# Hybrid decoder step on one core: attention outputs turned by transposes after a GpSimd add, in place of fp32 products with [I;I]

## The chip, the core and the metric

The kernel runs on one core of a Trainium2 chip. The metric is the device time of one launch in microseconds. The engines of the core are TensorE (PE; its weight loads are listed as PEld), VectorE (DVE), ScalarE (ACT), GpSimd (POOL) and SyncE (SP), each with its own queue of instructions; they wait for each other by semaphores.

## What is computed

One decoder layer over a prompt of 2048 positions and over 8 sequences of 8 new positions with a paged cache of 8192. The change touches the attention of the prompt alone: 8 heads of 64, causal, with a forget-gate term in the logits.

```python
def _attend_block(q, k, v, qc, kc, q_pos, k_pos):
    s = jnp.einsum('bqhd,bkhd->bhqk', q, k).astype(jnp.float32) * ATTN_SCALE
    s = s + jnp.swapaxes(qc, 1, 2)[..., :, None] - jnp.swapaxes(kc, 1, 2)[..., None, :]
    causal = (q_pos[:, None] >= k_pos[None, :])[None, None]
    s = jnp.where(causal, s, NEG_INF)
    p = jax.nn.softmax(s, axis=-1)
    return jnp.einsum('bhqk,bkhd->bqhd', p.astype(v.dtype), v)

# _layer
p = x @ w_in                      # q, k, v, forget gates, pooling channels
att = _forget_attention(...)      # 128 queries at a time
mix = concat(att, pool) @ w_out
x1 = layer_norm(ALPHA * x + mix)
x2 = layer_norm(ALPHA * x1 + conv_ffn(x1))
```

## The kernel before, in words

Stages run one after the other with a barrier of all engines between them: projection (A), gates and pooling (B), prompt attention (C), mixing and first norm (Dp), the feed-forward network with the decoding attention beside it (F, N), and the sampled rows (S). The change is in `stage_attention` (C).

It works on 32 groups (`groups`): a head `h` and a block `g` of 512 queries, four tiles of 128. Even heads take g = 0, 1, 2, 3, odd heads 3, 2, 1, 0, so that the lengths repeat every eight groups. A group has 4, 8, 12 or 16 turns, one for each tile of 128 keys (`turns`, `steps`, 320 in all). Orders are fixed by hand in each engine's block; two turns make a `pair`.

- TensorE: `logits` writes the products q.k of a coming group into PSUM (`ps_s`, lines 880 to 884); `transposes` turns tiles of the exponentials (`row`) so that keys lie on partitions (`ps_t`, line 896); `times_v` multiplies by the values into `ps_o` (lines 908 and 910), once with the rounded weights `p_hi` and once with the rest `p_lo`; `turn_back(n)` brings the group's output into rows of queries.
- VectorE: `copy_logits` (line 949) scales, copies and takes the least value; `rest` (line 961) forms `p_lo`; `normalise` (lines 968 to 978) multiplies the turned output by the reciprocal sum into `att`.
- ScalarE: `exp` (line 1005), `high` (line 1013, rounds to `p_hi`), and `o_out` (line 1019), the copy of `ps_o` to SBUF.
- GpSimd has nothing to do in this stage.

`v` holds, for each key, the 64 values of a head as a rounded part and a rest side by side, 128 columns. `ps_o` therefore has the rounded values' output on partitions 0 to 63 and the rest's on 64 to 127; their sum is the output. Before, `o_out` copies all 128 partitions to `oT` (in the persistent tile `raw0`, seen as `X_raw` in the profile), and `turn_back` multiplies each 128x128 block of `oT` by `both`, two 64x64 identities on top of each other: this fp32 product adds the halves and turns them at once, into 64 columns per tile of queries.

At the border between groups n and n+1, ScalarE waits in `o_out(n)` for the last `times_v` of n and copies; behind it stand exponentials and roundings of the coming turns. TensorE goes on with two turns of transposes and with logits, waits for the copy at the first `times_v` of n+1 (`o_copied`), does two turns of `times_v`, and then `turn_back(n)` (`nat_at`). VectorE's `normalise(n)` waits for it (`nat_done`). The buffers of `ps_t` are four and are used in turn (`t_free`).

## Time and profile before

| | us |
|---|---|
| median of 3 runs | 3110.25 (3105.86 to 3114.26) |
| span of the profiled execution | 3104.8 |
| TensorE busy | 2980.9 (96%) |
| VectorE busy | 2011.5 (65%) |
| ScalarE busy | 1554.0 (50%) |
| GpSimd busy | 810.0 (26%) |

The profile is of one execution; for it only the span is given, from its first to its last recorded instruction, and no time around it. Busy times are sums over the engine's instructions. Matmuls overlap in the records, since they are pipelined: a matmul lasts longer there than the distance to the next one. An idle time in square brackets behind a row is what the engine waited just before it, with the operation that ended the wait. The granted clock is a share of TensorE's full clock (1.0 is 2.4 GHz, 0.5 is 1.2 GHz), averaged over a stretch. The prompt attention spans about 481 to 966 us.

### The profile page before, as it was taken

Reading aid. Unit: us, or ns where it says so; the run is one execution under the profiler, and the core shown is the slowest. Engines: PE = TensorE matmul, PEld = TensorE weight load, DVE = VectorE, ACT = ScalarE, POOL = GpSimd, SP = SyncE. Lnnn points to the kernel's source line nnn. Section 1 sums busy time; section 2 is a strip of 40 time slices with the busy share of each in tenths; the row PEclk is TensorE's granted clock in tenths of the full one; section 3 lists DMA queues with packets and bytes.
Section 4 is the critical chain, followed back from the end, with each engine's and each line's share of the span. In section 5 each row is a group of like instructions: output and inputs, shape, how many; then the busy total and the mean of one; then the engine's idle time right before and its main releaser. Section 6 shows DMA issues by size and latency. Waiting matters only on the chain. (4 is left out here: it accounts for less than half of the span.)

```text
span 3104.8 us, 57063 instructions
## 1 busy us (share of the span) xinstructions
PE 2980.9 (96%) x19424; PEld 2376.2 (77%) x19424; DVE 2011.5 (65%) x4185; ACT 1554.0 (50%) x3113; POOL 810.0 (26%) x1437
## 2 busy tenths in 40 slices
PE   8999978999999997999999999999999999999988
PEld 8999966777777886777777777777777777777762
DVE  5433336787886655866678666678666678666445
ACT  3111115776775113466445666446676446766424
POOL 1101110000000103434444334454343454442300
PEclk9999988999999998999999999999999999999999
DMA  5444455322303356757877677787677887775868
GB/s 205 134 127 122 127 133 152 81 55 67 86 21 112 122 166 219 253 197 247 289 270 262 235 247 246 268 298 269 222 245 230 284 299 240 249 240 177 301 249 323
DMA packets 270120, 626.51 MB, mean 202 GB/s; under 512 B 52279, under 2 KB 116695, under 8 KB 261855
## 3 DMA queue, kind: packets, MB, share of 16 engines
q1 hardware_dynamic: 169271, 305.32, 30.9%
q0 software_dynamic: 93760, 296.83, 28.2%
q10 hardware_dynamic: 6800, 20.71, 2.1%
q8 instruction: 156, 2.56, 0.3%
q14 instruction: 133, 1.09, 0.1%
HBM read 555.52 MB, written 67.33 MB: 201 GB/s over the span
## 5 line engine op out<-in xcount | busy, mean ns | idle before, releaser
L1568 PE MATMUL F_ps_u<-X_x_hi,F_w_hi 128*128 128x512 f32 x1408 | 577.4, 410 | 10.9 <-DVE F_w_lo L1827 10.9
L1569 PE MATMUL F_ps_u<-X_x_lo,F_w_hi 128*128 128x512 f32 x1408 | 560.0, 398 | 0.0
L1570 PE MATMUL F_ps_u<-X_x_hi,F_w_lo 128*128 128x512 f32 x1408 | 559.8, 398 | 0.0
L1827 DVE TENSOR_TENSOR F_w_lo<-X_raw,F_w_hi 128x512 fp32r<-128x512 f32 x352 | 239.2, 681 | 269.9 <-ACT F_w_hi L1727 268.2
L2056 POOL DMA_DIRECT2D N_dec<-cache_k x512 | 278.1, 543 | 312.5 <-issue 192.9
L2096 POOL DMA_DIRECT2D N_dec<-cache_v x512 | 281.9, 551 | 285.0 <-issue 163.7
L1568 PEld LDWEIGHTS F_ps_u<-X_x_hi,F_w_hi 128*128 128x128 f32 x1408 | 266.7, 189 | 103.5 <-issue 34.9
L1727 ACT CAST F_w_hi<-X_raw 128x512 fp32r<-128x512 f32 x352 | 214.3, 609 | 256.0 <-PE F_ps_y L1570 230.8
L1884 DVE STREAM_TRANSPOSE N_dec<-N_dec 128x1024 f32<-128x1024 f32 x256 | 303.6, 1222 | 19.2 <-DMA N_dec<-cache_k 18.8
L1570 PEld LDWEIGHTS F_ps_u<-X_x_hi,F_w_lo 128*128 128x128 f32 x1408 | 266.3, 189 | 64.5
L1569 PEld LDWEIGHTS F_ps_u<-X_x_lo,F_w_hi 128*128 128x128 f32 x1408 | 267.3, 190 | 56.7
L1752 ACT ACTIVATE F_h<-F_ps_u,F_coef 128x512 f32<-128x512 f32 x176 | 121.3, 689 | 344.6 <-PE F_ps_u L1570 344.5
L949 DVE TENSOR_SCALAR_CACHE_REDUCE C_row<-C_ps_s 128x512 f32<-128x512 f32 (+2 forms) x320 | 185.7, 609 | 81.6 <-PE C_ps_s L881 62.8
L252 PE MATMUL A_ps_p<-A_w_hi,A_x_hi 128*128 128x412 f32 (+1 forms) x640 | 226.0, 353 | 0.0
L2066 POOL DMA_DIRECT2D F_forget<-sc_wT x256 | 137.4, 542 | 332.1 <-DVE F_tops L1918 329.9
L254 PE MATMUL A_ps_p<-A_w_hi,A_x_lo 128*128 128x412 f32 (+1 forms) x640 | 223.7, 349 | 0.0
L253 PE MATMUL A_ps_p<-A_w_lo,A_x_hi 128*128 128x412 f32 (+1 forms) x640 | 223.5, 349 | 0.0
L1827 DVE TENSOR_TENSOR F_w_lo<-F_raw,F_w_hi 128x512 fp32r<-128x512 f32 x176 | 119.3, 678 | 126.6 <-ACT F_w_hi L1727 126.0
L1294 POOL TENSOR_TENSOR H_qs<-Dp_pin,H_qs 128x512 fp32r<-128x512 f32 x16 | 23.2, 1449 | 681.5 <-ACT H_qs L1216 681.5
L1013 ACT CAST C_p_hi<-C_ps_t 128x512 fp32r<-128x512 f32 (+1 forms) x320 | 151.7, 527 | 93.0 <-PE C_ps_t L896 92.9
L1568 PE MATMUL F_ps_y<-F_w_hi,F_g_hi 128*128 128x512 f32 x480 | 197.6, 412 | 0.0
L1570 PE MATMUL F_ps_y<-F_w_hi,F_g_lo 128*128 128x512 f32 x480 | 190.1, 396 | 0.0
(345 smaller groups left out, 6388.3 us busy)
## 6 DMA issues: line engine op xcount, KB each, us to landing
N_dec<-cache_k POOLq DMA_DIRECT2D x512, 256.0 KB, 3.6
N_dec<-cache_v POOLq DMA_DIRECT2D x512, 256.0 KB, 4.7
X_raw<-w_up_t SPq DMA_DIRECT2D x120, 512.0 KB, 5.2
F_raw<-w_up_t SPq DMA_DIRECT2D x56, 512.0 KB, 5.0
X_raw<-w_down SPq DMA_DIRECT2D x56, 512.0 KB, 5.4
sc_qk<-A_early SPq DMA_DIRECT2D x16, 1024.0 KB, 5.1
F_forget<-sc_wT POOLq DMA_DIRECT2D x256, 64.0 KB, 3.0
F_raw<-w_down SPq DMA_DIRECT2D x32, 512.0 KB, 4.3
```

The costliest lines, as they stand in the source:

```text
L252: nc.tensor.matmul(out, x_hi[:, t % 2, c, :], w_hi[:, c, cols], start=c == 0, stop=False)
L253: nc.tensor.matmul(out, x_hi[:, t % 2, c, :], w_lo[:, c, cols], start=False, stop=False)
L254: last = nc.tensor.matmul(out, x_lo[:, t % 2, c, :], w_hi[:, c, cols], start=False, stop=c == DC - 1)
L949: nc.vector.tensor_scalar(row[:, n % 2, r, o:o + w], ps_s[:, p % SBANKS, 0:w], -SCALE, None, ALU.mult, ALU.min, accum_out=least[:, n % 4, ...
L1568: nc.tensor.matmul(out, a_hi, b_hi, start=first, stop=False)
L1569: nc.tensor.matmul(out, a_hi, b_lo, start=False, stop=False)
L1570: return nc.tensor.matmul(out, a_lo, b_hi, start=False, stop=last)
L1727: nc.scalar.copy(w_hi[:, q % 4, :], raw[unit % RAW][:, q % 2 * 512:(q % 2 + 1) * 512]).then_inc(hi_done, 1)
L1827: nc.vector.tensor_tensor(w_lo[:, q % 4, :], raw[q // 2 % RAW][:, q % 2 * 512:(q % 2 + 1) * 512], w_hi[:, q % 4, :].bitcast(F32), ALU.subt ...
L1884: nc.vector.transpose(kt[:, :, half % 2 * 64:(half % 2 + 1) * 64].rearrange("p f (j t) -> p j f t", j=2), kin[:, half % KR, :, :].rearrang ...
L2056: pool.dma_start(kin[:, half % KR, j, :], io["cache_k"][ds(pages[j], 1), :, :].rearrange("a t c -> (a t) c"))\
L2096: pool.dma_start(vin[j:P:4, n % 2, :, :], io["cache_v"][ds(pages[j], 1), :, :].rearrange("a (b t) c -> (a t) b c", b=4))\
```

## The change

`o_out` copies the two halves of `ps_o` apart, both to partitions 0 to 63: the first to `oT`, which now has 64 partitions, the second to the new tile `oT_low`. A GpSimd block, new in this stage, adds `oT_low` into `oT` for each group and signals `o_summed`. `turn_back` waits for that sum and turns it by four transposes with the 64x64 corner of the identity, which write the same 64 columns per tile as before. Between its two copies ScalarE waits until the sum of the group before is done, since `oT_low` has a single buffer. The tile `both`, its two loads and their semaphore go.

```diff
@@ stage_attention
-        oT = persist["raw"][0][:, :].rearrange("p (a d) -> p a d", a=2)
-        both = m.sb("both", [P, HD])
+        oT = persist["raw"][0][0:HD, :].rearrange("p (a d) -> p a d", a=2)
+        oT_low = m.sb("oT_low", [HD, 512])
...
         @block.sync
         def _(sp):
-            sp.dma_start(both[0:HD, :], io["c_ident"][0:HD, 0:HD]).then_inc(c_in, 16)
-            sp.dma_start(both[HD:P, :], io["c_ident"][0:HD, 0:HD]).then_inc(c_in, 16)
...
             def turn_back(n):
                 tk = nat_tick[n]
-                if n == 0:
-                    pe.wait_ge(c_in, 32)
-                pe.wait_ge(o_copied, n + 1)
+                pe.wait_ge(o_summed, n + 1)
                 pe.wait_ge(t_free, tk - TBANKS + 1)
                 for r in range(4):
-                    last = nc.tensor.matmul(ps_t[:, tk % TBANKS, r * HD:(r + 1) * HD], oT[:, n % 2, r * P:(r + 1) * P], both[:, :],
-                                            start=True, stop=True)
+                    last = nc.tensor.transpose(ps_t[:, tk % TBANKS, r * HD:(r + 1) * HD], oT[:, n % 2, r * P:(r + 1) * P],
+                                               ident[0:HD, 0:HD])
                 last.then_inc(nat_done, 1)
...
                 act.wait_ge(pv_done, first_t[n + 1])
                 if n >= 2:
                     act.wait_ge(nat_done, n - 1)
-                nc.scalar.copy(oT[:, n % 2, :], ps_o[:, :]).then_inc(o_copied, 1)
+                nc.scalar.copy(oT[:, n % 2, :], ps_o[0:HD, :])
+                if n:
+                    act.wait_ge(o_summed, n)
+                nc.scalar.copy(oT_low[:, :], ps_o[HD:P, :]).then_inc(o_copied, 1)
...
+        @block.gpsimd
+        def _(pool):
+            for n in range(NGR):
+                pool.wait_ge(o_copied, n + 1)
+                nc.gpsimd.tensor_tensor(oT[:, n % 2, :], oT[:, n % 2, :], oT_low[:, :], ALU.add).then_inc(o_summed, 1)
```

The built programs differ in the order of instructions at three places. The first is ScalarE's queue at the border behind group 3 (head 0, queries 1536 to 2047), before:

```order
L1005 ACTIVATE C_row,C_total<-C_row,C_lowest 128x1024
L1013 CAST C_p_hi<-C_ps_t 128x512 x2
L1019 COPY X_raw<-C_ps_o 128x512
L1005 ACTIVATE C_row,C_total<-C_row,C_lowest 128x640
L1005 ACTIVATE C_row,C_total<-C_row,C_lowest 128x768
L1013 CAST C_p_hi<-C_ps_t 128x512 x2
```

The same place in the changed kernel, where line numbers are a few lower up to here:

```order
L1001 ACTIVATE C_row,C_total<-C_row,C_lowest 128x1024
L1009 CAST C_p_hi<-C_ps_t 128x512 x2
L1015 COPY X_raw<-C_ps_o 64x512
L1018 COPY C_oT_low<-C_ps_o 64x512
L1001 ACTIVATE C_row,C_total<-C_row,C_lowest 128x640
L1001 ACTIVATE C_row,C_total<-C_row,C_lowest 128x768
L1009 CAST C_p_hi<-C_ps_t 128x512 x2
```

A second copy stands ahead of the exponentials and the next roundings; nothing else moved. The second place is TensorE's queue behind the same border, at `turn_back`, before:

```order
L908 MATMUL C_ps_o<-C_p_hi,C_v 128x512
L910 MATMUL C_ps_o<-C_p_lo,C_v 128x512
L920 MATMUL C_ps_t<-C_both,X_raw 128x64 x4
L896 MATMUL C_ps_t<-all_ident,C_row 128x128 x8
L880 MATMUL C_ps_s<-H_ks,H_qs 128x512
```

And in the changed kernel:

```order
L906 MATMUL C_ps_o<-C_p_hi,C_v 128x512
L908 MATMUL C_ps_o<-C_p_lo,C_v 128x512
L916 MATMUL C_ps_t<-all_ident,X_raw 128x64 x4
L894 MATMUL C_ps_t<-all_ident,C_row 128x128 x8
L878 MATMUL C_ps_s<-H_ks,H_qs 128x512
```

The four operations keep their place; their second operand is now the identity. The third place is GpSimd's queue between the gates stage and the mixing stage, in the changed kernel:

```order
L739 MEMSET X_x_lo 4x4096 [waits A_l_in0]
L526 UNCONDITIONAL_BRANCH
L65 ISA [waits barrier_Pool_Activation_PE_DVE_SP_gather]
L1033 UNCONDITIONAL_BRANCH [waits barrier_Pool_Activation_PE_DVE_SP_gather]
L1037 TENSOR_TENSOR X_raw<-X_raw,C_oT_low 64x512 [waits A_p_dve] x32
L822 UNCONDITIONAL_BRANCH
```

Before, no arithmetic stood between the two stages' barriers there; now the 32 adds do.

## Rows read from the trace of the kernel before

**Rows 1.** Busy time of each engine by stretches (us, instructions), granted clock, DMA share, GB/s.

```profile
485.00:966.00 481.00, 453.06 (x2740) 368.53 (x2740) 384.34 (x1130) 330.99 (x730) 0.00 (x0) 0.97 0.27 66
613.27:623.64 10.37, 7.66 (x40) 6.35 (x39) 5.45 (x19) 6.08 (x13) 0.00 (x0) 0.84 0.29 103
```

**Rows 2.** Groups by shape, 485 to 966 us: busy us, mean ns, idle before.

```profile
L961 DVE TENSOR_TENSOR C_p_lo<-C_ps_t,C_p_hi 128x512 fp32r<-128x512 f32 x224 | 144.7, 685 | 1.2 <-ACT C_p_hi L1013 1.0
L1013 ACT CAST C_p_hi<-C_ps_t 128x512 fp32r<-128x512 f32 x224 | 122.0, 590 | 82.0 <-PE C_ps_t L896 82.0
L920 PE MATMUL C_ps_t<-C_both,X_raw 128*128 128x64 f32 x256 | 32.1, 268 | 0.7 <-ACT X_raw L1019 0.7
```

**Rows 3.** Timeline of TensorE, 436 to 437 us: start, us, what [idle before].

```profile
436.20 0.46 PE L307 MATMUL A_ps_t<-all_ident,A_prow 64*128 64x64 f32 x4 [0.59 <-ACT A_prow L337]
436.59 0.63 PE L311 MATMUL A_ps_t<-all_ident,A_early 120*128 120x120 f32 x4
```

**Rows 4.** Groups by shape, ScalarE, whole span.

```profile
L2274 ACT COPY S_hrow<-S_ps_h 64x512 f32<-64x512 f32 x1 | 0.6, 579 | 2.1 <-PE S_ps_h L2238 2.1
```

**Rows 5.** Lines 1294 and 1255 (mixing stage): duration ns min/median/max, first and last start.

```profile
L1294 POOL TENSOR_TENSOR H_qs<-Dp_pin,H_qs x16: 1279/1289/1928, 974.5 to 1154.5; 128x512 fp32r<-128x512 f32 x16
L1255 DVE TENSOR_TENSOR H_qs<-Dp_ps_a,H_qs x16: 682/691/692, 968.7 to 1154.0; 128x512 fp32r<-128x512 f32 x16
```

**Rows 6.** Timelines of ScalarE, VectorE, TensorE and its weight loads at border 4.

```profile
679.08 0.59 ACT L1019 COPY X_raw<-C_ps_o 128x512 f32<-128x512 f32 x1 [0.72 <-PE C_ps_o L910]
679.56 0.83 ACT L1005 ACTIVATE C_row<-C_row,C_lowest 128x640 f32<-128x640 f32 x1
...
681.30 1.06 ACT L1013 CAST C_p_hi<-C_ps_t 128x512 fp32r<-128x512 f32 x2
...
681.46 1.00 PE L920 MATMUL C_ps_t<-C_both,X_raw 128*128 128x64 f32 x8
...
681.90 1.29 DVE L961 TENSOR_TENSOR C_p_lo<-C_ps_t,C_p_hi 128x512 fp32r<-128x512 f32 x2
...
682.30 1.04 PE L896 MATMUL C_ps_t<-all_ident,C_row 128*128 128x128 f32 x8
...
687.13 0.19 PEld L908 LDWEIGHTS C_ps_o<-C_p_hi,C_v 128*128 128x128 f32 x1 [0.18 <-DVE C_p_lo L961]
```

**Rows 7.** Timeline behind borders 1, 2, 3, 5 and 6.

```profile
630.44 0.69 DVE L949 TENSOR_SCALAR_CACHE_REDUCE C_row<-C_ps_s 128x512 f32<-128x512 f32 x1 [0.18 <-PE C_ps_s L881]
...
644.18 0.69 DVE L949 TENSOR_SCALAR_CACHE_REDUCE C_row<-C_ps_s 128x512 f32<-128x512 f32 x1 [0.37 <-PE C_ps_s L881]
...
661.18 0.42 PEld L896 LDWEIGHTS C_ps_t<-all_ident,C_row 128*128 128x128 f32 x4 [0.15 <-DVE C_p_lo L961]
...
706.69 0.69 DVE L949 TENSOR_SCALAR_CACHE_REDUCE C_row<-C_ps_s 128x512 f32<-128x512 f32 x1 [0.33 <-PE C_ps_s L881]
...
717.50 0.97 ACT L1013 CAST C_p_hi<-C_ps_t 128x512 fp32r<-128x512 f32 x2 [0.66 <-PE C_ps_t L896]
```

**Rows 8.** Timeline behind border 7, and one row behind border 8.

```profile
722.89 0.58 ACT L1019 COPY X_raw<-C_ps_o 128x512 f32<-128x512 f32 x1 [1.50 <-PE C_ps_o L910]
...
724.83 1.00 PE L920 MATMUL C_ps_t<-C_both,X_raw 128*128 128x64 f32 x8
...
726.14 0.75 PEld L896 LDWEIGHTS C_ps_t<-all_ident,C_row 128*128 128x128 f32 x7 [0.45 <-ACT C_row L1005]
...
737.07 0.86 PEld L896 LDWEIGHTS C_ps_t<-all_ident,C_row 128*128 128x128 f32 x8 [1.73 <-ACT C_row L1005]
```

**Rows 9.** Timeline of the stage's end: the last two copies and their products.

```profile
960.75 0.60 ACT L1019 COPY X_raw<-C_ps_o 128x512 f32<-128x512 f32 x1
...
962.39 1.00 PE L920 MATMUL C_ps_t<-C_both,X_raw 128*128 128x64 f32 x8
...
963.90 0.58 ACT L1019 COPY X_raw<-C_ps_o 128x512 f32<-128x512 f32 x1 [2.09 <-PE C_ps_o L910]
...
964.53 1.10 PE L920 MATMUL C_ps_t<-C_both,X_raw 128*128 128x64 f32 x8 [0.68 <-ACT X_raw L1019]
```

More of the change, by code:

```diff
@@ L837, in stage_attention @@
         v_in = [m.sem("v_in0"), m.sem("v_in1")]
-        c_in, logf_out = m.sem("c_in"), m.sem("logf_out")
+        logf_out = m.sem("logf_out")
         s_done, s_copied, least_ready, exp_done = m.sem("s_done"), m.sem("s_copied"), m.sem("least_ready"), m.sem("exp_done")
         t_done, hi_done, t_free, pv_done = m.sem("t_done"), m.sem("hi_done"), m.sem("t_free"), m.sem("pv_done")
-        o_copied, nat_done, rec_ready = m.sem("o_copied"), m.sem("nat_done"), m.sem("rec_ready")
+        o_copied, o_summed, nat_done, rec_ready = m.sem("o_copied"), m.sem("o_summed"), m.sem("nat_done"), m.sem("rec_ready")
         summed = m.sem("summed")
```

## The prediction

> **What bounds the kernel now.** I read the busy shares first, then the stretch that the change touches, then the waits inside it. The prompt attention runs from about 481 to 966 us. In 481 us of it TensorE is busy for 453.06, VectorE for 384.34, ScalarE for 331.0 and GpSimd for nothing [rows 1]. So TensorE leads, and work taken from it can shorten the stage, but only where it isn't waiting for another engine. The costliest shapes show who these are: ScalarE rounds a transposed tile of weights (`high`, line 1013, 590 ns) and VectorE takes the rest (line 961, 685 ns), 224 times each at full width [rows 2]. TensorE, ScalarE and VectorE hand each tile on in turn, so a delay of ScalarE can come back to TensorE. What matters is what happens at the 32 borders between groups, where `o_out` and `turn_back` stand. The pattern of borders repeats every eight groups (a pair of heads, groups of 4, 8, 12, 16, 16, 12, 8, 4 key tiles); I number the borders 1 to 8 after the group that ends, and read heads 2 and 3 (623 to 742 us).
>
> **TensorE's part.** The four fp32 products with [I;I] are recorded as eight instructions per border, 256 in all [rows 2]; at border 4 the next work starts 0.84 us behind their first [rows 6]. Four transposes of a 64-row tile by a 64x64 identity stand in the trace already: line 307, and the line behind it starts 0.39 us later [rows 3]. Saved are 0.84 - 0.39 = 0.45 us per border, 32 x 0.45 = 14.4 us of TensorE's work in all. The bounds: nothing saved, or all 0.84 (27 us); I take 0.45, since line 307 is the same shape.
>
> **ScalarE's part.** One copy of 128x512 becomes two of 64x512. A 64x512 copy out of PSUM takes 0.6 us, 579 ns by its mean [rows 4], and the 128x512 one at border 4 takes 0.59 [rows 6]: half the partitions save nothing. Back to back a copy costs less than it lasts: behind the copy at 679.08 the next operation starts at 679.56, 0.48 us later [rows 6]. So all that stands behind `o_out` on ScalarE (exponentials, and the rounding of the next tiles) moves by 0.48 us per border, 15.4 us of work in all. The bounds are 0 (ScalarE was going to idle anyway) and 0.6. The first `times_v` of the next group waits for the second copy too, but at border 4 it has one round of transposes and logits ahead of it, so this wait costs little. The added wait for `o_summed` of the group before stands between the copies; that sum is at least one whole group old, so I cost it at nothing, save in the case below where the add is very slow.
>
> **GpSimd's part.** The sum is a new step between the copy and `turn_back`. The nearest row is line 1294, an add of two SBUF tiles 128x512: median 1.289 us, longest 1.928 [rows 5]; for 64 partitions I take the same 1.29, bounded by 0.65 (half) and 1.93. From the first copy's start the sum is ready after 0.48 + 0.59 + 1.29 and about 0.05 for each of two hand-overs, 2.46 us. TensorE now reaches `turn_back` 681.46 - 679.08 = 2.38 us after the copy's start at border 4 [rows 6] and 724.83 - 722.89 = 1.94 after it at border 7, the tightest [rows 8]. So it would wait 0.1 and 0.5 us, about what the shorter transposes give back. Borders 1 to 3 have more room.
>
> **VectorE's part.** It keeps its instructions. Normalisation waits for `nat_done`, which comes at 2.46 + 0.39 instead of 1.94 + 1.0 at border 7: no later. Could the add slow VectorE? In the mixing stage line 1255 reads PSUM and one SBUF tile, as line 961 does; its 16 runs, in the same 186 us as the 16 adds of line 1294, all take 682 to 692 ns [rows 5]. So I cost this at nothing.
>
> One rule speaks against this change. The row of the add has 1.29 us where VectorE's line 1255, as wide, has 0.69 [rows 5]. The Trainium skill ("GPSIMD Engine Reference", Performance versus the Vector engine, and Engine selection) wants elementwise adds on VectorE, since GpSimd takes about twice as long with two inputs; the trace agrees. Its 4,497 ns for 2,048 columns make, as an estimate by that page, 1.12 us for 512: the sum would be ready 0.17 us sooner and the total 0.3 us lower, by the two adds at the end of the stage.
>
> **Where it lands, border by border.** At each I ask what TensorE waits for next after `turn_back`, and whether VectorE or ScalarE can follow a TensorE that is 0.45 us early [rows 7].
> - Border 1: VectorE later idles 0.18 us for logits, then TensorE waits for VectorE. The gain is limited to 0.18.
> - Border 2: VectorE idles 0.37 for logits: gain 0.37.
> - Border 3: the second round of transposes already waits 0.15 us for VectorE (its buffer): TensorE being early is lost, gain 0.
> - Border 4: behind the copy ScalarE is busy without a break, and its rounding at 681.30 ends just before VectorE's rest starts at 681.90; the chain goes on through VectorE to the product at 687.13, which waits for it [rows 6]. ScalarE's 0.48 comes out on TensorE: loss 0.48.
> - Border 5: VectorE idles 0.33 for logits: gain 0.33.
> - Border 6: ScalarE idles 0.66 before its next rounding, which takes up the 0.48; the chain through VectorE is tight, gain 0.1.
> - Borders 7 and 8: TensorE waits 0.45 and 1.73 us for the exponentials that stand behind the copy on ScalarE [rows 8]. It is the ScalarE chain that ends this wait: loss 0.48 at each, and nothing for shorter transposes.
>
> Per pair of heads borders 1 to 6 give 0.18 + 0.37 + 0 - 0.48 + 0.33 + 0.1 = +0.5 us, four times: 2.0 us gained. Borders 7 and 8 lose 0.96, three times: 2.9 us. The fourth time they are the end of the stage, where nothing hides the chain: the last copy starts at 963.90 and its products at 964.53 [rows 9]. The sum is ready 2.46 us after the copy, 1.83 later than the products start now; less 0.45 that is 1.4. The group before adds the same kind of wait, 960.75 + 2.46 = 963.21 against 962.39, less 0.45: 0.4 (the copy of that group starts at 960.75 [rows 9]). End: 1.8 us. The two removed loads of the identity are issued beside other loads before the stage's first products; nobody waits for them before the first `turn_back`: 0.
>
> Sum: - 2.0 + 2.9 + 1.8 = +2.7 us, from a span of 3104.8 to 3107.5. The three plain runs have their median at 3110.25, 5.4 us above this span, and I carry that difference over: **3113 us**. A measurement of this kernel can tell about 0.3%, 9.3 us, from no change; this is well inside.
>
> **Rivals.**
> 1. *TensorE's time comes through.* If VectorE and ScalarE follow (each is idle for 97 and 150 of the 481 us [rows 1]), 28 borders give 0.45 us each, 12.6, less 1.8 at the end: 3110 - 11 = 3099. Against it: the tight hand-overs of [rows 6] and [rows 8]. It would need ScalarE's second copy to be hidden nearly everywhere. If the transposes were cheaper than I think (the 0.84 bound), 3091. Chance 0.13.
> 2. *The add is late (slower).* TensorE stands still in `turn_back` with everything behind it. With 1.93 us the sum is ready at 3.1 us, and borders 4 to 7 would wait 0.6 to 1.2 us, of which some 0.9 us per pair of heads isn't given back: +3.6, 3117, still no change. From an add (with its hand-overs) of about 2.5 us on, each further us costs four or five borders of each pair their full wait, some 16 us per us, and the time passes 3120. For it: GpSimd spans are the roughest in the profile, and 1.93 did occur. Chance 0.12.
> 3. *ScalarE's delay comes through everywhere (slower).* 32 x 0.48 = 15.4, plus 1.8: 3127. Against it: ScalarE waits for transposes behind most borders, as for 0.66 us in [rows 7]. Chance 0.09.
> 4. *The add slows VectorE after all.* If each of the 32 adds stretched what runs beside it by a fifth of 1.29 us, that is 8 us: 3121. Chance 0.03.
> 5. *The clock.* After border 8, with TensorE waiting, the granted clock was 0.84 of full speed on average in the 10.4 us from 613.27 on, so part of it at 1.2 instead of 2.4 GHz [rows 1]. Longer waits there may lengthen such stretches: at 0.84 over 10.4 us no more than 1.7 us of work is lost each time, so twice that long costs 5 us in all, 3118. The Trainium skill ("TensorE: Matmul & The Clock Gate", PE-mode transpose) says that transposes don't count as activity for the clock as products do, which would favour this case. Chance 0.03.
> 6. *The transposes save nothing* (an operation of the same eight passes). Then borders 1, 2, 5 and 6 give nothing: +4, and waits for the sum aren't paid back: 3118. Chance 0.05.
>
> **How the numbers follow.** My forecast has 0.55: 3103 to 3119. Faster by over 0.3% (under 3101) is rival 1 and a little of the forecast's edge: 0.14. Slower by over 0.3% (over 3119.6) takes rivals 2 and 3 nearly whole and part of 4 to 6: 0.24. Within: 0.62. The range must leave out no more than 2 in 10: from 3100 (the near part of rival 1) to 3124 (the add at its bound together with some of ScalarE's delay, and most of rival 4).
>
> **What would show it.** In the changed profile: line 1037 on GpSimd near 1.3 us; the two ScalarE copies near 0.58 each, 0.48 apart; four transposes per border, 128 instructions, taking 0.4 us; waits of TensorE for GpSimd at borders 4 to 8; the waits for exponentials at borders 7 and 8 grown to about 0.9 and 2.2 us; the stage longer by about 2 to 3 us and its end later by 1.8. I would be wrong if a pair of heads, from the copy that ends its border 1 to that of the next pair, came out more than 2 us shorter or longer than now.

## The result and the profile after

The changed kernel takes 3122.3 us (median of 5 runs, 3121.6 to 3127.5) where the kernel before has 3110.25 in the runs beside it. The ratio is 1.0044 [1.0031, 1.0058]: slower by 0.44%, past the 0.3% that a measurement can tell. A second series gave 3122.7 us and 1.0043 [1.0029, 1.0057]. The forecast was 3113, no change; the time lies inside the range (3100 to 3124), near its upper end. The profiled execution took 3122.28 us with a span of 3120.6, against a span of 3104.8 before.

The new operations, over the whole span (duration in ns min/median/max, first and last start, forms):

```profile
L1015 ACT COPY X_raw<-C_ps_o x32: 579/580/583, 503.7 to 973.5; 64x512 f32<-64x512 f32 x32
...
L1018 ACT COPY C_oT_low<-C_ps_o x32: 582/583/587, 504.3 to 974.1; 64x512 f32<-64x512 f32 x32
...
L1037 POOL TENSOR_TENSOR X_raw<-X_raw,C_oT_low x32: 1254/1286/1297, 505.0 to 974.8; 64x512 f32<-64x512 f32 x32
...
L916 PE MATMUL C_ps_t<-all_ident,X_raw x128: 221/223/366, 508.2 to 976.4; 64*128 64x64 f32 x128
```

Each cost about what the forecast said: the copies 0.58, the add 1.29 and never more than 1.30, and the work behind `turn_back` starts 0.39 us after the first of its four transposes (border 4: 682.89 and 683.28). Busy time in 485 to 966 us, to be set beside [rows 1], and the stretch from the first border to the last one in each kernel (us, PE, PEld, DVE, ACT, POOL, granted clock, DMA share, GB/s), after and then before:

```profile
485.00:966.00 481.00, 442.73 (x2571) 346.37 (x2571) 379.92 (x1117) 346.99 (x750) 38.57 (x30) 0.96 0.27 66
505.00:975.00 470.00, 433.87 (x2540) 339.42 (x2538) 373.61 (x1091) 343.81 (x744) 40.06 (x32) 0.97 0.24 58
```

```profile
505.00:966.00 461.00, 436.67 (x2683) 355.84 (x2681) 374.61 (x1095) 323.48 (x714) 0.00 (x0) 0.99 0.24 59
```

The window up to 966 cuts off the last 9 us of the changed kernel's stage, so the stretches from border to border are the ones to compare: TensorE is busy for 2.8 us less (433.87 against 436.67) in a stretch 9 us longer, and stands still for 36.1 us instead of 24.3. And there is a second thing, in the column of the clock: 0.97 against 0.99. Which waits grew is in the waits of the two kernels for the same stretches (us in total, times, longest), after and then before:

```profile
PE C_ps_t L894 <- ACT C_row L1001: 14.5, 18, 2.6
PE C_ps_o L906 <- DVE C_p_lo L957: 7.9, 15, 1.1
PE C_ps_o L906 <- ACT C_oT_low L1018: 4.1, 4, 1.1
PE C_ps_t L894 <- DVE C_p_lo L957: 3.9, 8, 0.7
PE C_ps_t L916 <- POOL X_raw L1037: 1.1, 5, 0.2
```

```profile
PE C_ps_o L908 <- DVE C_p_lo L961: 10.4, 18, 1.1
PE C_ps_t L896 <- ACT C_row L1005: 10.0, 18, 1.6
PE C_ps_o L908 <- ACT X_raw L1019: 0.5, 1, 0.5
```

TensorE waits 4.5 us longer for exponentials. It waits 3.6 us longer for the accumulator, which the products of the next group may not touch until the second copy has read it; part of that stood as a wait for VectorE before, which is 2.5 us shorter. All four of these waits are at borders 7; the prediction had looked at this wait at border 4 alone. New is also a wait of 3.9 us, 0.3 at each border 3 and 0.66 at each border 4, for VectorE to free a buffer of transposed weights. The wait for the sum is small inside the stage, 1.1 us in all. Here are the waits at a border 7, to be set beside [rows 8] (start, us, engine, line, what, idle before):

```profile
724.78 0.58 ACT L1015 COPY X_raw<-C_ps_o 64x512 f32<-64x512 f32 x1 [1.52 <-PE C_ps_o L908]
...
725.37 0.58 ACT L1018 COPY C_oT_low<-C_ps_o 64x512 f32<-64x512 f32 x1
...
725.97 0.54 ACT L1009 CAST C_p_hi<-C_ps_t 128x256 fp32r<-128x256 f32 x2
726.03 1.28 POOL L1037 TENSOR_TENSOR X_raw<-X_raw,C_oT_low 64x512 f32<-64x512 f32 x1 [7.79 <-ACT C_oT_low L1018]
...
726.09 0.47 PE L906 MATMUL C_ps_o<-C_p_hi,C_v 128*128 128x512 f32 x1 [1.00 <-ACT C_oT_low L1018]
...
727.36 0.46 PE L916 MATMUL C_ps_t<-all_ident,X_raw 64*128 64x64 f32 x4 [0.21 <-POOL X_raw L1037]
...
728.75 0.44 PE L894 MATMUL C_ps_t<-all_ident,C_row 128*128 128x128 f32 x2 [0.93 <-ACT C_row L1001]
...
740.38 1.97 PE L894 MATMUL C_ps_t<-all_ident,C_row 128*128 128x128 f32 x8 [2.61 <-ACT C_row L1001]
```

(The last row is behind the border 8 that follows.) The sum ends 2.53 us after the copy's start and `turn_back` starts on it at 2.58 (forecast 2.46, hand-overs included), after a wait of 0.21 us. But it is the row at 728.75 that sets the time: transposes of the weights start 728.75 - 724.78 = 3.97 us after the copy, 726.14 - 722.89 = 3.25 before [rows 8], and the 0.72 between them is ScalarE's: its rounding starts 1.19 us after the first copy. (In "two copies only" below, with products in `turn_back` and no sum, they start after 3.97 us as well.) The clock shows where border 7 goes wrong in the next pair of heads, from its copy to that of border 8 (same columns as above), after and then before:

```profile
845.72:858.84 13.12, 10.97 (x44) 8.47 (x43) 7.63 (x27) 4.94 (x15) 1.28 (x1) 0.64 0.63 132
```

```profile
843.28:852.49 9.21, 8.05 (x48) 5.68 (x47) 6.70 (x26) 4.17 (x14) 0.00 (x0) 1.00 0.90 187
```

3.9 us are lost on one border. 0.7 of them are lost at the border 7 of the second pair too, where the clock stays full; the other 3.2 go with a mean clock of 0.64 of full speed in this stretch, where before it was 1.00. Seven transposes of weights take 1.76 us there:

```profile
849.69 1.76 PE L894 MATMUL C_ps_t<-all_ident,C_row 128*128 128x128 f32 x7 [0.93 <-ACT C_row L1001]
```

```profile
846.53 0.98 PE L896 MATMUL C_ps_t<-all_ident,C_row 128*128 128x128 f32 x7 [0.31 <-ACT C_row L1005]
```

For all borders I took the start of each copy in both traces (in the changed kernel that of the first copy) and how much longer the way to the next one has become. "Second pair" is heads 2 and 3, whose borders 7 and 8 have no more half clock than before (3.4 us, where before had 6.8); the last row is the sum over a whole pair.

| us after minus before | forecast | second pair | other three pairs |
|---|---|---|---|
| border 1 | -0.18 | -0.16 | -0.29, -1.12, +0.48 |
| border 2 | -0.37 | -0.28 | -0.29, -0.27, -0.24 |
| border 3 | 0 | +0.13 | +0.10 to +0.12 |
| border 4 | +0.48 | +0.68 | +0.66 to +0.71 |
| border 5 | -0.33 | -0.01 | -0.01 to +0.01 |
| border 6 | -0.1 | -0.01 | -0.01 to -0.04 |
| border 7 | +0.48 | +0.71 | +1.97, +3.92, +0.55 |
| border 8 | +0.48 | +0.49 | +0.58, +1.74, end of stage |
| pair | +0.46 | +1.55 | +2.79, +5.01, +1.51 |

(Border 1 varies because half-clock stretches of the one or the other kernel reach into it.) By the sign that I had set for being wrong, more than 2 us on a pair of heads, two of the three whole pairs say so, both by what half clock adds to them. From the first copy to the last it is 469.8 us instead of 458.9: +10.9. From the last copy to the first product of the mixing stage it is +1.5 (rows of the changed kernel and of the one before):

```profile
978.03 1.94 PE L1160 MATMUL Dp_ps_a<-all_ident,CD_att 128*128 128x128 f32 x8 [1.29 <-PEq L66]
```

```profile
966.92 1.94 PE L1155 MATMUL Dp_ps_a<-all_ident,CD_att 128*128 128x128 f32 x8 [1.28 <-PEq L66]
```

Of the 15.8 us by which the two spans differ the rest lies in code that the change doesn't touch: +5.5 from there to about 1345 us, part of it beside stretches of half clock, and -0.8 behind that, less 1.3 because the first copy came earlier.

### The profile page after: what moved, and what is told of

Read it like the earlier page. It is cut to its first block and busy times, and to the rows that moved or that the text cites. A ratio compares the mean times of both kernels' runs of the same rounds, so it can differ in the third digit from the quotient of the medians.

```text
span 3120.6 us, 56869 instructions
## 1 busy us (share of the span) xinstructions
PE 2975.3 (95%) x19296; PEld 2356.3 (76%) x19296; DVE 2010.7 (64%) x4185; ACT 1575.7 (50%) x3145; POOL 851.5 (27%) x1469
## 5 line engine op out<-in xcount | busy, mean ns | idle before, releaser
L1574 PE MATMUL F_ps_y<-F_w_lo,F_g_hi 128*128 128x512 f32 x480 | 189.0, 394 | 0.0
```

Source lines behind the costliest of these rows:

```text
L1574: nc.tensor.matmul(out, a_hi, b_lo, start=False, stop=False)
```

## The experiments

Where nothing else is said an edit is against the kernel before. The theory was that ScalarE's second copy, with what follows from it, is the cost, and that the add is nearly hidden; the rivals were the add (late, or a hindrance to VectorE), transposes that save nothing, and the clock. Ratios are against the kernel before, in runs beside it. The last column is of one profiled execution each, with its own stretches of half clock, and not of the median one.

| kernel | median us | ratio | first to last copy, us more than before |
|---|---|---|---|
| changed kernel, again | 3122.7 | 1.0043 [1.0029, 1.0057] | +11.9 |
| transposes only | 3108.3 | 1.0003 [0.9993, 1.0012] | -0.8 |
| two copies only | 3125.7 | 1.0061 [1.0047, 1.0075] | +14.4 |
| add only | 3113.5 | 1.0015 [1.0006, 1.0025] | +0.4 |
| changed, products kept | 3127.4 | 1.0064 [1.0051, 1.0078] | +15.8 |
| changed, `turn_back` later | 3133.0 | 1.0067 [1.0053, 1.0081] | +19.4 |
| full-width copy twice | 3120.6 | 1.0044 [1.0030, 1.0057] | +9.2 |
| add behind the turn | 3107.7 | 0.9999 [0.9990, 1.0008] | -3.3 |
| changed, filled with products | 3113.9 | 1.0016 [1.0007, 1.0025] | +1.3 |
| changed, filled with transposes | 3113.8 | 1.0016 [1.0006, 1.0025] | +2.2 |
| add behind, filled | 3107.3 | 0.9995 [0.9986, 1.0004] | -5.8 |
| before, filled | 3107.2 | 0.9995 [0.9986, 1.0004] | -3.4 |

### One part at a time

**Transposes only.** They read the upper 64 rows; the lower half isn't added, that part of the result is left out.

```diff
-                    last = nc.tensor.matmul(ps_t[...], oT[:, n % 2, r * P:(r + 1) * P], both[:, :], start=True, stop=True)
+                    last = nc.tensor.transpose(ps_t[...], oT[0:HD, n % 2, r * P:(r + 1) * P], ident[0:HD, 0:HD])
```

> The kernel before, with one change: turn_back is four exact transposes of the upper 64 partitions of oT. ScalarE keeps its one copy of 128x512, GpSimd has nothing to do. Left out: the lower half of each output (the product with the rest of v) isn't added. My theory after the result (T): the second ScalarE copy and the wait for the add took more than the shorter transposes give, and the transposes alone give little, since VectorE or ScalarE is behind TensorE at most borders: 0.18 + 0.37 + 0.33 + 0.1 us per pair of heads and 0.9 at the end, 5 us in all: 3105. Rival R1 (TensorE's time comes through): 32 x 0.45 = 14 us less, 3096. Rival C (transposes don't keep the clock up): extra stretches at half clock in the attention, as in the changed kernel, and a time at or above 3110.

No change: 1.0003, and 3 us over the 3105 that I had expected. Borders 3 to 5 and 7 move by less than 0.1 us (save the last of them), border 2 gains 0.25 to 0.28, border 6 0.12 to 0.15. Border 5, where I had counted on 0.33, gains nothing. Where the 0.45 us go stands at border 7 of the second pair (timeline of TensorE, then the row of the kernel before):

```profile
725.53 0.46 PE L920 MATMUL C_ps_t<-all_ident,X_raw 64*128 64x64 f32 x4
...
726.75 0.98 PE L896 MATMUL C_ps_t<-all_ident,C_row 128*128 128x128 f32 x7 [0.76 <-ACT C_row L1005]
```

```profile
726.14 0.98 PE L896 MATMUL C_ps_t<-all_ident,C_row 128*128 128x128 f32 x7 [0.32 <-ACT C_row L1005]
```

The wait behind the transposes is 0.76 us, where the row of before has 0.32: the 0.44 saved is waited out. This settles the first rival (TensorE's time comes through): it does not, even with nothing added on ScalarE.

**Two copies only.** Two copies of 64 partitions each, to their own partitions; products with [I;I] as before.

```diff
-                nc.scalar.copy(oT[:, n % 2, :], ps_o[:, :]).then_inc(o_copied, 1)
+                nc.scalar.copy(oT[0:HD, n % 2, :], ps_o[0:HD, :])
+                nc.scalar.copy(oT[HD:P, n % 2, :], ps_o[HD:P, :]).then_inc(o_copied, 1)
```

> The kernel before, with one change: o_out copies the two halves of ps_o by two ScalarE copies of 64 partitions each, to their own partitions of oT; products with [I;I], no add, no further wait. T: the copies stand 0.48 us apart (0.59 in the changed kernel, where a wait stands between them), borders 4, 7 and 8 and the end pay it: about 4 x 1.4 us, 3116. Rival R2 (only the wait for the add pays): 3110 to 3111. Rival R3 (ScalarE's delay comes through everywhere): 32 x 0.5, 3126.

3125.7 us, ratio 1.0061, some 10 us more than I expected; the cost of the whole change and more is in this one edit (what its own stretches of half clock cost is in it). Its timeline of ScalarE at border 4:

```profile
681.67 0.58 ACT L1019 COPY X_raw<-C_ps_o 64x512 f32<-64x512 f32 x1 [0.76 <-PE C_ps_o L910]
682.26 0.58 ACT L1020 COPY X_raw<-C_ps_o 64x512 f32<-64x512 f32 x1
682.87 0.83 ACT L1005 ACTIVATE C_row<-C_row,C_lowest 128x640 f32<-128x640 f32 x1
```

The second starts 0.59 after the first, and the exponentials 0.61 after that: 1.20 from first copy to exponentials, where it was 679.56 - 679.08 = 0.48 [rows 6]. So the exponentials come 0.72 us later, not 0.48, and border 4 costs +0.8, border 7 +0.7 where the clock stays full. In the changed kernel these are 1.08 and 0.60:

```profile
680.29 0.58 ACT L1015 COPY X_raw<-C_ps_o 64x512 f32<-64x512 f32 x1 [0.76 <-PE C_ps_o L908]
680.89 0.58 ACT L1018 COPY C_oT_low<-C_ps_o 64x512 f32<-64x512 f32 x1
681.37 0.83 ACT L1001 ACTIVATE C_row<-C_row,C_lowest 128x640 f32<-128x640 f32 x1
```

Here too the second copy follows after 0.6, though it has a wait for the sum of the group before ahead of it: that wait costs nothing. But the exponentials follow the second half copy after 0.48. And at borders 7, where a rounding stands behind it, that one follows after 0.60.

**Add only.** GpSimd adds the upper half to itself into a spare tile that nobody reads; `turn_back` waits for it.

```diff
+                nc.gpsimd.tensor_tensor(o_sum[:, :], oT[0:HD, n % 2, :], oT[0:HD, n % 2, :], ALU.add).then_inc(o_summed, 1)
...
-                pe.wait_ge(o_copied, n + 1)
+                pe.wait_ge(o_summed, n + 1)
```

> The kernel before, with one change: GpSimd adds the upper half of oT to itself into a spare tile of 64x512 after each copy, and turn_back waits for this add; one copy, products with [I;I]; the add's result isn't used. The add is ready about 0.59 + 0.07 + 1.29 + 0.05 = 2.0 us behind the copy's start, TensorE comes at 1.94 to 2.5 us at borders 4 to 8. T: next to no wait but at the stage's end (1.4 + 0.4 us), 3112; a larger time means that an add by itself costs (its port, its semaphores, or the clock). Rival R2 (the add's lateness is the main cost): 3118 or more.

3113.5 us, ratio 1.0015 [1.0006, 1.0025], where I had expected 3112. In the trace nothing moves at the borders (each within 0.1 us save the few beside half-clock stretches), so the add slows neither VectorE nor anything else there; what it costs in the trace is at the end of the stage, where TensorE stands for it:

```profile
961.97 0.59 ACT L1021 COPY X_raw<-C_ps_o 128x512 f32<-128x512 f32 x1 [2.32 <-PE C_ps_o L912]
962.63 1.03 POOL L1042 TENSOR_TENSOR C_o_sum<-X_raw 64x512 f32<-64x512 f32 x1 [2.32 <-ACT X_raw L1021]
...
963.72 1.39 PE L922 MATMUL C_ps_t<-C_both,X_raw 128*128 128x64 f32 x8 [1.78 <-POOL C_o_sum L1042]
```

From copy to products it is 1.75 us against 0.63 [rows 9]; from the last copy to the first product of the mixing stage +1.4. The ratio says 4.7 us, and the trace is of the fastest of ten executions (3107.9 us, mean clock 0.982; the slowest took 3119.3 at 0.978), so some 3 us of the median aren't in it, and their cause isn't shown. This add is a little cheaper than the real one (1.03 against 1.29, it reads one tile twice) and starts 0.6 us sooner after the copy, so it bounds rivals 2 and 4 from below only.

**The changed kernel with products.** Only the fourth part of the change is taken back: `matmul` with the 64x64 identity for `transpose`.

```diff
-                    last = nc.tensor.transpose(ps_t[...], oT[:, n % 2, r * P:(r + 1) * P], ident[0:HD, 0:HD])
+                    last = nc.tensor.matmul(ps_t[...], oT[:, n % 2, r * P:(r + 1) * P], ident[0:HD, 0:HD], start=True, stop=True)
```

> The changed kernel with one step back: turn_back uses fp32 products with a 64x64 identity in place of exact transposes; two copies, the add and all waits stay. It measures the transposes inside the changed kernel. T: transposes there give back 0.45 us only at borders where TensorE is ahead of nobody (2, 5, 6 and the end), 1 to 1.5 us per pair of heads: 3122 + 5 = 3127. If the transposes gave nothing: 3122. If all: 3122 + 14 = 3136. If transposes lower the clock: below 3122, and fewer stretches at half clock than in the changed kernel's trace.

3127.4 us, as expected: 5 us more than the changed kernel. Against that kernel borders 1, 2, 5 and 6 are longer by 0.5, 0.6, 0.33 and 0.65 us. Rival 6 (transposes save nothing) falls. But this isn't quite the old cost of `turn_back` put back (border 2):

```profile
647.50 1.10 PE L916 MATMUL C_ps_t<-all_ident,X_raw 64*128 64x64 f32 x8
648.54 1.09 PE L894 MATMUL C_ps_t<-all_ident,C_row 128*128 128x128 f32 x8
```

The next work starts 1.04 us behind the first product of 64 rows, where it is 0.84 with [I;I] [rows 6] and 0.39 with transposes. So the 5 us are a price against these dearer products; against those of the kernel before, the transposes are worth less within the change, and "two copies only", which has the old products and no add, is 3 us above the changed kernel. Nor is a wait for the sum what they give back at borders 1 and 2: there `turn_back` starts 4.5 and 3.9 us after the copy, and the sum is ready after 2.5. At border 6 the sum does hold it, to 2.59 us after the copy, where it was 2.21.

### The copy, its width and its clock

**Full-width copy twice.** The whole accumulator is copied to a spare tile, then to its place. Nothing else is changed.

```diff
+                nc.scalar.copy(spare[:, :], ps_o[:, :])
                 nc.scalar.copy(oT[:, n % 2, :], ps_o[:, :]).then_inc(o_copied, 1)
```

> The kernel before with its copy of 128x512 made twice, first into a spare tile, then into oT; nothing else changed. It measures what a second copy costs when both are of 128 partitions. In the changed kernel the two copies of 64 partitions stand 0.59 us apart and the exponentials start 1.08 us after the first, where one copy of 128 lets them start after 0.48. Theory S64 (64-partition copies don't overlap what follows as others do): here the copies stand 0.48 apart, exponentials start after 0.96, and the time is some 2 us under that of the kernel with two half copies (3125.7). Rival: any two copies out of this one PSUM tile stand 0.59 apart; then the time is that of the two half copies, 3124 to 3126. If ScalarE's delay were not the cause at all: 3108 to 3110.

3120.6 us, ratio 1.0044: 5 us under the two half copies, where I had expected 2. Its ScalarE at border 4:

```profile
685.21 0.59 ACT L1020 COPY C_spare<-C_ps_o 128x512 f32<-128x512 f32 x1 [0.72 <-PE C_ps_o L911]
685.69 0.59 ACT L1021 COPY X_raw<-C_ps_o 128x512 f32<-128x512 f32 x1
686.17 0.84 ACT L1006 ACTIVATE C_row<-C_row,C_lowest 128x640 f32<-128x640 f32 x1
```

Each adds exactly 0.48 us, and the borders show it: 4 costs +0.42 to +0.46 and 7 costs +0.47 to +0.49. So my reading of ScalarE's step was right for 128 partitions, and a second half copy doesn't follow the first as closely: 0.59 instead of 0.48. Full width is no dearer than half: 586 ns against 580.

**`turn_back` later.** NAT_AFTER, the number of transposed pairs of tiles after which `turn_back` stands, is 3 instead of 2.

```diff
-    PAIRS, NAT_AFTER = NTR // 2, 2
+    PAIRS, NAT_AFTER = NTR // 2, 3
```

> The changed kernel with NAT_AFTER 3 in place of 2: turn_back and normalise stand one pair of turns later, so the add is ready long before. Theory S: only TensorE's waits for GpSimd go (some 10 us of waits in all, of which borders 4 to 8 get back at most 0.5 us each where TensorE is not waiting for ScalarE or VectorE anyway), the ScalarE delay stays: 0 to 4 us less than the changed kernel, 3119 to 3123. Rival R2 (the late add is the cost): 3110 to 3112, all of it gone save the end.

I had expected up to 3123 us, and it took 3133 in the median. The runs of this one kernel went from 3122.1 to 3133.5, and they sort by the granted clock: the one at 3122.1 has a mean of 0.980 over the span, the four from 3129.9 up have 0.974. Its profile is one of those (stretches):

```profile
505.00:985.00 480.00, 440.73 (x2549) 345.77 (x2547) 373.74 (x1092) 345.11 (x746) 40.64 (x32) 0.95 0.23 57
732.40:759.70 27.30, 24.19 (x86) 19.48 (x86) 13.67 (x47) 11.78 (x24) 2.54 (x2) 0.50 0.29 75
```

For 27 us around borders 7 and 8 TensorE runs at 0.50, which is 1.2 GHz. Borders 3 and 5 also cost 0.4 and 0.5 us more than in the changed kernel, so a later place is no cure for the wait, and this run was the first to say that the clock is a term of several us.

**Filled with products or with transposes.** In the changed kernel, idle work on TensorE ahead of the waits for exponentials behind borders 7 and 8 (rows 728.75 and 740.38 above): 8 small operations at the one and 22 at the other, into a bank that the real work overwrites. They are products in the one kernel and transposes in the other. The wait for a free bank moves ahead of the idle work.

```diff
+            FILL = (8, 22)
+            def fill(bank, times):
+                for _ in range(times):
+                    nc.tensor.matmul(ps_t[:, bank, 0:P], identb[:, :], causal[:, :], start=True, stop=True)
...
+                if k == 0 and n >= 8 and n % 8 < 2:
+                    fill(tk % TBANKS, FILL[n % 8])
                 if k * P % HALF == 0:
                     pe.wait_ge(exp_done, exps_until(n, k * P // HALF))
```

> The changed kernel with idle work for TensorE: before the first transposes of a group that wait for exponentials behind borders 7 and 8 (where it stands still for 0.93 and 2.61 us in the changed kernel's trace), it makes 8 and 22 bf16 products of 128x128 with the identity into the bank that those transposes then overwrite. Theory K (some 4 of the 12 to 14 us are longer stretches of half clock, brought on by longer pauses of TensorE at borders 7 and 8): less than 10 us at half clock between 505 and 965 us, where the changed kernel's two traces have 31 each, and a time of 3116 to 3119. Rival (the low stretches have another cause, or cost nothing since TensorE waits there): 3122 or more.

> The same as its neighbour e9, with fp32 transposes of the identity in place of the bf16 products, 8 and 22 again (about 0.1 us each, as the transposes of this kernel). It asks whether transposes keep the clock up as products do. The Trainium skill (TensorE: Matmul & The Clock Gate, PE-mode transpose) says that transposes don't count as activity in the way products do: by that rule the low stretches stay at some 31 us and the time at 3122 to 3124. If they count: as e9, 3116 to 3119.

Stretches of the kernel filled with products, and then of that filled with transposes:

```profile
505.00:960.00 455.00, 425.23 (x2615) 331.37 (x2613) 371.23 (x1085) 340.14 (x737) 38.51 (x30) 1.00 0.24 60
720.00:760.00 40.00, 34.15 (x221) 25.21 (x220) 28.43 (x94) 24.56 (x56) 5.11 (x4) 1.00 0.37 87
```

```profile
505.00:966.00 461.00, 434.99 (x2638) 340.84 (x2638) 374.38 (x1092) 343.13 (x744) 39.25 (x31) 1.00 0.24 59
720.00:760.00 40.00, 35.90 (x224) 27.04 (x223) 28.03 (x92) 24.71 (x58) 3.85 (x3) 1.00 0.44 105
```

Both hold the full clock through all inner borders, and both take 3114 us, where I had expected 3116 to 3119: 8.6 us less than the changed kernel, for work that computes nothing. (The two weren't run beside each other; by their ratios it is 8.7 us, give or take 5.) What the waits cost stays as it was (border 4 +0.65 to +0.70, border 7 +0.71 to +0.73, the last one 0.55). So the clock is worth these 8.6 us, against 5 us that rival 5 had given to it.

It doesn't matter which operation fills. By the rule of the Trainium skill ("TensorE: Matmul & The Clock Gate", PE-mode transpose: a transpose doesn't count for the clock as a product does) the transposes ought to have left the clock low. The measurement decides: here, between products, they kept it at 1.00 as the products did. A long stretch of transposes alone was not run.

**Before, filled.** The same fill (4 and 16 products) in the kernel before.

> The kernel before with 4 and 16 bf16 products of idle work at the same two places (TensorE waits 0.45 and 1.73 us there). Theory K: its 13.7 us at half clock between 505 and 965 us shrink to a few, worth about a third of that, 3 us: 3104 to 3106. Rival: no change, 3108 to 3110.

3107.2, 0.9995 [0.9986, 1.0004]: the kernel before has little to win here (0.99 becomes 1.00), less than I had expected, and the interval holds no change at all. That gives a price for the change with the clock taken out of both in this stage: 3113.9 - 3107.2 = 6.8 us, give or take 4. In the two traces +4.8 are between the first copy and the last. Border by border these two kernels differ by +0.70 at 4, +0.72 at 7 and +0.72 at 8 in the second pair, -0.30 and -0.25 at 1 and 2, and less than 0.05 at the rest.

### Another way to the same end

**Add behind the turn.** One full-width copy, transposes of 128x128; VectorE normalises both halves (128 columns instead of 64 for each of the four), and GpSimd adds them into `att`. Against the changed kernel:

```diff
-                nc.scalar.copy(oT[:, n % 2, :], ps_o[0:HD, :])
-                if n:
-                    act.wait_ge(o_summed, n)
-                nc.scalar.copy(oT_low[:, :], ps_o[HD:P, :]).then_inc(o_copied, 1)
+                nc.scalar.copy(oT[:, n % 2, :], ps_o[:, :]).then_inc(o_copied, 1)
...
-                    last = nc.tensor.transpose(ps_t[...], oT[:, n % 2, r * P:(r + 1) * P], ident[0:HD, 0:HD])
+                    last = nc.tensor.transpose(ps_t[...], oT[:, n % 2, r * P:(r + 1) * P], ident[:, :])
...
+                nc.vector.tensor_tensor(turned[:, :, :], ps_t[...], rec[...].to_broadcast([P, 4, P]), ALU.mult).then_inc(t_free, 1)
...
+                nc.gpsimd.tensor_tensor(att[...], turned[:, :, 0:HD], turned[:, :, HD:P], ALU.add).then_inc(added, 1)
```

> A version meant to keep the gain without the costs: one copy of 128x512 as before, four exact 128x128 transposes, VectorE multiplies all 128 columns per tile by the reciprocal into a spare tile (0.69 us in place of 0.42, 32 times), and GpSimd adds the two halves into att behind it, where only the stage's end waits. Theory S: no second copy, so nothing at borders 4, 7 and 8 but 0.27 us of VectorE; TensorE is 0.45 us shorter at each border, of which little shows, as in the kernel with transposes alone (ratio 1.0003); the end pays one add of 128x256, about 0.7 us: 3108 to 3112, below the changed kernel by 12 us. Rival (any use of GpSimd or of transposes here costs): 3118 or more.

0.9999 [0.9990, 1.0008], no change, as expected: 14 to 15 us better than the changed kernel, and no better than the one before. Its exact transposes stay, the second copy is gone, and nobody on TensorE waits for the add. The same with fill (8 and 20 products):

> The version with one copy, exact transposes and the GpSimd add behind VectorE (e8, ratio 0.9999), with 8 and 20 bf16 products of idle work at the same two places. Theory K: the low stretches between 505 and 965 us go (6.8 us of them in e8's trace), and the spread of e8's runs (3103 to 3113) narrows to its lower half: 3101 to 3105, which would beat both kernels. Rival: the filler delays the waiting transposes, or the clock's falls there cost nothing: 3107 or more.

0.9995 [0.9986, 1.0004]. In its trace the last copy stands 5.8 us nearer to the first one than before, and yet the median is 0.8 us shorter and no more. I had expected 3101 to 3105. Its profiled execution (span 3106.2) gave the gain back in later stages, 3.3 us of it near 2614 us beside a stretch at half clock; this is one execution, and why it fell so isn't settled.

## Why the prediction came out as it did

The range held the time; "no change" didn't. The sum was +2.7 us, and 12 to 14 came. That the time is inside is luck: the upper end of 3124 was drawn for an add at its bound with some more of ScalarE's delay, and for a slowed VectorE, but the add took what was forecast, VectorE was not slowed, and most of the miss is the clock. The step that failed is the one from the delay of ScalarE to time on TensorE: each delay was priced by its own length, a little too short, and without what it does to the clock.

- **What bounds it.** Right: TensorE leads by its busy time and can't be made faster by itself here, since ScalarE and VectorE hand it each tile. "Transposes only" shows it: 1.0003.
- **The prices of single operations.** Right, all of them: add 1.29 and 1.29, transposes 0.39, copies 0.58, `turn_back` free to start after 2.46 forecast and 2.58 measured, nothing for the wait between the two copies. "VectorE nothing" holds too: line 957 has 684 ns where [rows 2] have 685, with the adds beside it:

```profile
L957 DVE TENSOR_TENSOR C_p_lo<-C_ps_t,C_p_hi 128x512 fp32r<-128x512 f32 x222 | 143.2, 684 | 3.1 <-ACT C_p_hi L1009 3.0
```

- **ScalarE's second copy, 0.48 us.** The term that was mis-sized. I read the step of 0.48 from a copy of 128 partitions followed by an activation [rows 6]. "Two copies only" and "full-width copy twice" tell that a second copy starts after 0.59 if both have 64 partitions and after 0.48 if both have 128. I had given 0.6 as the bound, and took the row that looked nearest.
- **Borders 1 to 3.** Right within 0.13 us, in the second pair and where no half clock reaches in.
- **Borders 4, 7 and 8, +0.48 each.** Right in place and direction, and 0.2 too small: 0.68, 0.71 and 0.72 (8 by the two filled kernels; the +0.49 in the table is against a longer half-clock stretch of before). Border 7 is fully in the rows: there two steps of 0.59 and 0.60 come ahead of ScalarE's rounding, 1.19 us, where one of 723.38 - 722.89 = 0.49 did before, +0.70. The row 723.38 belongs to the kernel before:

```profile
723.38 0.55 ACT L1013 CAST C_p_hi<-C_ps_t 128x256 fp32r<-128x256 f32 x2
```

  The accumulator, which the second copy holds, delays the products there too, but the exponentials end later still. At border 4 0.60 of the 0.68 are so explained. There the delay doesn't reach TensorE at the product that I had named, but earlier, 4.31 us after the copy, where transposes wait for VectorE to free their buffer (no such wait in the kernel before):

```profile
684.60 0.65 PE L894 MATMUL C_ps_t<-all_ident,C_row 128*128 128x128 f32 x4 [0.66 <-DVE C_p_lo L957]
```

- **Borders 5 and 6, -0.33 and -0.1.** Border 5 failed, and in its reading. I had read the gain from the logits for which VectorE idles [rows 7]. "Transposes only" has TensorE out of `turn_back` 0.36 us earlier than before and no sum to wait for, and this border gains 0.00 there; in it and in the changed kernel `turn_back` starts at the same 2.63 us after the copy. "Products kept", where TensorE comes out of `turn_back` 0.28 us later than before, costs +0.33 (all counted from the copy). So TensorE has nothing to spare there and nothing to win. What it had become earlier is waited out at the weights of the transposes behind, for VectorE to free their buffer, as I had it for border 3 ("transposes only"; 0.33 in the changed kernel, no such wait before):

```profile
703.86 0.42 PEld L896 LDWEIGHTS C_ps_t<-all_ident,C_row 128*128 128x128 f32 x4 [0.34 <-DVE C_p_lo L961]
```

  Border 6 gave its 0.1 alone (0.12 to 0.15) and 0.01 to 0.04 in the change, where `turn_back` has to wait for the sum.
- **The end, +1.8.** Right for the last copy, for which 1.4 of it stood: +1.5 to the first product of the mixing stage. The wait for the sum is as forecast (2.60 us on TensorE):

```profile
973.50 0.58 ACT L1015 COPY X_raw<-C_ps_o 64x512 f32<-64x512 f32 x1 [1.95 <-PE C_ps_o L908]
...
974.75 1.25 POOL L1037 TENSOR_TENSOR X_raw<-X_raw,C_oT_low 64x512 f32<-64x512 f32 x1 [2.40 <-ACT C_oT_low L1018]
...
976.06 0.69 PE L916 MATMUL C_ps_t<-all_ident,X_raw 64*128 64x64 f32 x4 [2.60 <-POOL X_raw L1037]
```

  From copy to `turn_back` it is 2.56 us against 0.63 [rows 9], +1.93 where I had 1.83. The transposes themselves take 0.69 instead of 0.46 there, at half clock. Another 1.9 us are lost in the first 25 us of the mixing stage; with the changed kernel run again nothing more is lost there, so I don't count them to the change.
- **Together, without the clock.** The two filled kernels differ by 6.8 us, give or take 4: 4.8 between the copies by their traces, where the forecast has -2.0 + 2.9 + 0.4 = 1.3, and 2.0 left for the rest, where it has 1.4. The 3.5 us between 1.3 and 4.8 are 2.5 for the borders 4, 7 and 8, 1.3 for the borders 5, 1.1 for 2, 3 and 6, less 1.3 at the borders 1, most of it half clock at the first of them.
- **The clock, rival 5.** This is the largest failure: I gave it 5 us and a chance of 0.03, as a rival that excludes the main one. The fillers price it at 8.6 us in the changed kernel and 0.9 in the one before, so 7.7 come with the change (give or take 6, since four medians go into it), on top of the waits. [rows 1] had shown a mean of 0.84 behind border 8 already in the kernel before. Between 505 and 965 us there are 13.7 us at half clock in the trace before and 30.7 in that of the changed kernel. What the fillers show is that this goes when TensorE has something to do ahead of the waits at borders 7 and 8. I had forecast 0.9 and 2.2 us for these waits from the rows of the weight loads [rows 8]; there they came out as 1.07 and 2.75, on TensorE itself they grew from 0.32 to 0.93 and from 1.59 to 2.61. I counted a wait of 0.5 us as 0.5 us, and it had its own price attached.
- **The other rivals.** 1 (TensorE's time comes through) and 6 (transposes save nothing) are refuted by their own kernels. The 3091 given under 1 is also a slip of its sum: 28 times 0.84 less 1.8 is 21.7 us, about 3088. 2 (add late): it did not take 1.9 us once. 3 (ScalarE's delay everywhere) gave a time not far off, 3127, by the wrong mechanism: at borders 1, 2, 5 and 6 the delay was hidden. 4: VectorE was not slowed.

What the change is worth can so be divided: the second copy costs the most (alone 1.0061, its share of the clock included), the transposes win back 3 to 5 us of it, the add is hidden in the traces except at the end, and of the final 0.44% about half (0.21) is waiting and half (0.23) TensorE's clock at borders 7 and 8, each known to 0.15 or 0.2 points.

No version beats the kernel before by more than the measurement can tell. The best are "add behind the turn", the same with fill, and the kernel before with fill, at 0.9995 to 0.9999. A second buffer for the lower half, which was not tried, promises nothing: the wait that it would take away costs nothing (0.6 us between the two copies with it and without it).

## What to carry to other kernels

- Look at the granted clock by stretches before pricing a wait. Where it already falls below 1.00 behind a wait of TensorE, a longer wait costs more than its length (here about 8 us more for waits that had grown by 0.6 and 1.0 us, at six borders), and a few idle operations ahead of the wait give it back.
- Splitting an instruction across partitions isn't free where its time goes by columns: a copy of 64x512 takes ScalarE 580 ns and one of 128x512 586, so two half-height copies cost it twice one full one. If halves must meet, let them meet where they lie in the same partitions, behind the transpose.
- Making the busiest engine's work shorter does nothing where its next instruction waits for another engine: follow each saved piece to the next wait.

## What the runs showed of the hardware

- ScalarE: a copy from PSUM of 64x512 takes 580 ns and one of 128x512 586. A second copy starts 0.59 us after the first if both have 64 partitions, 0.48 if both have 128. Height alone doesn't decide what follows: exponentials start 0.61 us after the second half copy in "two copies only" and 0.48 after that of the changed kernel, which writes to partitions 0 to 63. What costs the 0.11 isn't separated.
- GpSimd: adding 64x512 with two inputs takes 1,286 ns, and the add of 128x512 in the mixing stage 1,289 [rows 5]: height costs nothing. In "add behind the turn" the same number of sums, laid out in 128 partitions, costs not much more than half:

```profile
L1035 POOL TENSOR_TENSOR CD_att<-C_turned x32: 722/735/747, 514.4 to 964.4; 128x256 f32<-128x256 f32 x32
```

- TensorE's clock at 1.2 GHz for 3 to 27 us at a time at borders whose waits are 0.9 to 2.6 us, in a stage of which it is busy for 92%; and one and the same kernel (`turn_back` later) with a mean clock of 0.980 or 0.974 from run to run, 3122 or 3133 us.
- Idle transposes between products kept that clock up as well as idle products did (1.00 from 505 to 966 us, 3113.8 and 3113.9 us).
